# Gate columns of a hybrid layer computed in other places of the program: out of the first projection, into the joins and the last gated-delta steps

## The reference, cut to what matters

```python
h = rms_norm(x, norm_g[layer])
cols = split_columns(h @ w_in[layer])      # 'gate' is the first 1024 of 3448 columns
y_gdn = gdn_branch(cols, ...)              # gated delta rule, both directions
y_mla = mla_branch(cols, ...)
y_rwkv = rwkv7_branch(cols, ...)
mix = concatenate([y_gdn, y_mla, y_rwkv]) * silu(cols['gate'])
x = x + mix @ w_out[layer]
```

```python
u = u0_c - w_c @ s
o = qg_c @ s + p_c @ u
s = ge_c * s + kd_c.T @ u
```

## Time and profile before

| what | value |
|---|---|
| median of 3 runs | 4808.96 us (4803.95 to 4815.57) |
| the profiled execution, its own time | 4815.59 us |
| its span, first to last instruction | 4813.8 us |
| mean granted TensorE clock | 0.893 |
| TensorE (PE) busy | 4066.1 us, 84% |
| VectorE (DVE) busy | 2108.3 us, 44% |
| ScalarE (ACT) busy | 1239.2 us, 26% |
| GpSimd (POOL) busy | 275.6 us, 6% |

### The profile page before, as it was taken

The page is one execution under the profiler, slowest core; times in us unless marked ns, Lnnn a source line. Parts: engine busy times, 40 slices in busy tenths (PEclk is TensorE's granted clock), DMA queues, the critical chain, the costliest instruction groups (busy, mean ns, idle before and its releaser), DMA issues. The chain is left out here.

```text
span 4813.8 us, 51714 instructions
## 1 busy us (share of the span) xinstructions
PE 4066.1 (84%) x20488; PEld 2632.0 (55%) x20488; DVE 2108.3 (44%) x3647; ACT 1239.2 (26%) x2039; POOL 275.6 (6%) x236
## 2 busy tenths in 40 slices
PE   6847887898879694788789887849999999899999
PEld 4336634775664443663477565437777666344443
DVE  1266136554454127613665445325666667200001
ACT  2043134423332114313442434131111111210002
POOL 0011000000000001100000000001122111000000
PEclk9977698887999896779887898979999999999999
DMA  3220102112012212020301202231111110311120
GB/s 122 70 100 27 65 26 68 36 50 83 7 46 105 95 64 93 27 69 26 89 22 40 83 7 77 95 101 36 40 40 40 36 40 9 131 35 40 39 83 35
DMA packets 270405, 276.38 MB, mean 57 GB/s; under 512 B 11808, under 2 KB 241312, under 8 KB 270128
## 3 DMA queue, kind: packets, MB, share of 16 engines
q1 hardware_dynamic: 270192, 273.44, 17.2%
HBM read 199.54 MB, written 78.05 MB: 58 GB/s over the span
## 5 line engine op out<-in xcount | busy, mean ns | idle before, releaser
L3151 PE MATMUL ps<-hT,wr 128*128 128x512 f32 x768 | 333.2, 596 | 19.6 <-DMA wr<-in_w_in 19.6
L2940 DVE SCALAR_TENSOR_TENSOR cv<-glu,params,cv 128x1024 f32<-128x1024 f32 x240 | 338.5, 1410 | 6.1
L491 PE MATMUL ps<-hT,w_cols_g 128*128 128x512 f32 x576 | 261.9, 616 | 71.5 <-PEq L156 71.5
L3151 PEld LDWEIGHTS ps<-hT,wr 128*128 128x128 f32 x768 | 146.8, 191 | 205.3 <-issue 184.8
L491 PEld LDWEIGHTS ps<-hT,w_cols_g 128*128 128x128 f32 x576 | 113.7, 199 | 217.3 <-issue 217.3
L2337 PE MATMUL ps<-kT,qs 96*128 96x512 f32 x384 | 199.9, 650 | 34.2 <-DVE qs L2395 34.2
L2613 PE MATMUL ps<-w_out,mT 128*128 128x512 f32 x512 | 222.4, 593 | 0.0
L491 PE MATMUL ps<-hT,w_cols 128*128 128x512 f32 x448 | 196.1, 600 | 29.4 <-PEq L156 29.4
L2359 PEld LDWEIGHTS ps<-V,pT 128*128 128x128 f32 x1536 | 184.9, 192 | 56.5 <-issue 41.4
L3271 DVE TENSOR_TENSOR zs<-zs,ps 128x1024 f32<-128x1024 f32 x16 | 19.5, 1221 | 407.7 <-PE ps L3151 407.7
L2359 PE MATMUL ps<-V,pT 128*128 128x64 f32 x1536 | 183.5, 273 | 13.3 <-DVE om L2393 11.6
(11 more groups left out here) (478 smaller groups left out, 7452.9 us busy)
## 6 DMA issues: line engine op xcount, KB each, us to landing
fh<-hT_hbm SPq DMA_DIRECT2D x32, 512.0 KB, 4.5
x<-x_hbm SPq DMA_DIRECT2D x25, 512.0 KB, 6.9
w_cols_g<-in_w_in SPq DMA_DIRECT2D x24, 512.0 KB, 3.8
wr<-in_w_in SPq DMA_DIRECT2D x24, 512.0 KB, 3.8
hT_hbm<-hT SPq DMA_DIRECT2D x2, 4096.0 KB, 13.2
kb_raw_w<-kb_hbm SPq DMA_DIRECT2D x32, 256.0 KB, 3.2
hT<-hT_hbm SPq DMA_DIRECT2D x2, 4096.0 KB, 13.0
gate_in<-gate_hbm SPq DMA_DIRECT2D x8, 1024.0 KB, 8.4
```

What stands on the lines that cost most here:

```text
L491: m = pe.matmul(ps[:, 2 * (n % 3) + b, :], lhsT=wc[:, k, :], rhs=hT[:, k, P + b * 512:P + (b + 1) * 512], start=(k == 0), stop=(k == KD - 1))
L2940: vec.scalar_tensor_tensor(out=cv[:, h % 2, :], in0=src, scalar=w, in1=cv[:, h % 2, :], op0=ALU.mult, op1=ALU.add).then_inc(*VEC(f"tap{h}_ ...
L3151: q = pe.matmul(ps[:, two_banks(j) + b, :], lhsT=wr[:, j % NW, k, :], rhs=x_in[:, k, b * HALF:(b + 1) * HALF], start=(k == 0), stop=(k == ...
```

## The change

The gate product of 256 columns leaves `front`, with its weights' load, its copy and its store. The narrow product has two banks instead of one, and ScalarE computes the scales of group 1 before it copies narrow tiles 0 and 1. In `gdn_chunk` six fills instead of eight stand before each join, and the products of the other two stand one by one between the join's small products, one ahead of every three of those. The 256 gate columns are computed in steps 4 to 7, two tiles in each (`last_columns`, 8 products a tile), in four parts per step: four products ahead of `second_half`, four ahead of `to_state`, eight ahead of `out_of_chunk`. In steps 0 to 3 the turned keys are made after both `diff`, and VectorE makes kd of them after `across` instead of before it.

```diff
@@ front
                         scales(0)
+                        scales(1)
                         narrow(0)
                         narrow(1)
-                        scales(1)
                         scales(2)
@@ front, tensor
-                        narrow(0)
-                        narrow(1)
                         for t in range(NT):
+                            narrow(t)
                             if t + 2 < NT:
                                 turn(t + 2)
-                            gate(t)
-                            if t + 2 < NT:
-                                narrow(t + 2)
@@ TURNS
-                        TURNS += [f"gam{s + 1}", f"kt{s}", f"d{s + 4}_0", f"d{s + 4}_1", f"q{s}_0", f"q{s}_1", f"g{s + 4}_0", f"o{s}", f"g{s + 4}_1"]
+                        TURNS += [f"gam{s + 1}", f"d{s + 4}_0", f"d{s + 4}_1", f"kt{s}", f"q{s}_0", f"q{s}_1", f"g{s + 4}_0", f"o{s}", f"g{s + 4}_1"]
                     TURNS += ["pc1_0", "pc1_1", "of1_0", "of1_1"]
                     for s in range(4, NT):
-                        TURNS += ([f"gam{s + 1}"] if s < NT - 1 else []) + [f"kt{s}", f"q{s}_0", f"q{s}_1", f"o{s}"]
+                        TURNS += ([f"gam{s + 1}"] if s < NT - 1 else []) + [f"kt{s}", f"q{s}_0", f"q{s}_1", f"o{s}", f"f{s}"]
@@ new function, tensor
+                            def last_columns(s, part):
+                                b = claim(f"f{s}") if part == 0 else pair_of_banks(f"f{s}")
+                                n = 2 * NT + 2 * (s - 4) + part // 2
+                                if part == 0:
+                                    pe.wait_ge(*DMA.upto("fw", 3))
+                                if part % 2 == 0:
+                                    pe.wait_ge(*DMA.upto(f"fh{n % 2}", n // 2 + 1))
+                                for k in range(4 * (part % 2), 4 * (part % 2) + 4):
+                                    q = pe.matmul(ps[:, b + part // 2, 0:REST], lhsT=fh[:, n % 2, k, :], rhs=fw[:, k, 0:REST], start=(k == 0), stop=(k == KD - 1))
+                                if part % 2:
+                                    q.then_inc(*PE(f"fill{n}"))
@@ join, the same in its second half with NT * b + NT - 1
                                     for n in range(12):
+                                        if n % 3 == 0:
+                                            fill(NT * b + NT - 2, 4 * hf + n // 3, 4 * hf + n // 3 + 1)
                                         q = pe.matmul(ps[:, at, 32 * n:32 * n + 32], lhsT=AT5[:, 12 * hf + n, :], rhs=G[:, 0, :, 12 * hf + n], start=True,
@@ steps 0 to 3, tensor
                                 decays(s + 1)
-                                keys(s)
                                 diff(s + 4, 0)
                                 first_half(s)
                                 diff(s + 4, 1)
+                                keys(s)
                                 across(s)
@@ steps 4 to 7, tensor
                                 out_of_state(s)
+                                last_columns(s, 0)
                                 second_half(s)
                                 if s < NT - 1:
                                     values_in(s + 1)
+                                last_columns(s, 1)
                                 to_state(s)
+                                last_columns(s, 2)
+                                last_columns(s, 3)
                                 out_of_chunk(s)
@@ scalar: a copy of both tiles at once, after second_half and before out
+                            def last_columns(s):
+                                n = 2 * NT + 2 * (s - 4)
+                                act.wait_ge(*PE[f"fill{n + 1}"])
+                                for m in range(2):
+                                    act.wait_ge(*DMA.upto(f"fo{m}", n // 2))
+                                b = pair_of_banks(f"f{s}")
+                                act.copy(fo[:, :, 0:REST], ps[:, b:b + 2, 0:REST]).then_inc(*ACT(f"f{s}"))
@@ sync: the weights of the last columns are loaded behind the last fill, and their tiles two ahead
+                                    if n == NT * (c + 1) - 1:
+                                        fill_weights(c + 1)
+                                    fill_tile(n + 2)
```

More of the change, by code:

```diff
@@ L436, in _ @@
                         turned(1)
-                        for t in range(NT):
-                            if t + 2 < NT:
-                                normed(t + 2)
-                                turned(t + 2)
-                            gate(t)
+                        for t in range(2, NT):
+                            normed(t)
+                            turned(t)
                     @block.tensor
@@ L455, in narrow @@
                             pe.wait_ge(*VEC[f"h{t}_1"])
-                            if t:
-                                pe.wait_ge(*ACT[f"tm{t - 1}"])
+                            if t >= 2:
+                                pe.wait_ge(*ACT[f"tm{t - 2}"])
                             for k in range(KD):
-                                q = pe.matmul(ps[:, NARROW, 0:TM_W], lhsT=hT[:, k, (t + 1) * P:(t + 2) * P], rhs=wt[:, k, :], start=(k == 0), stop=(k == KD - 1))
+                                q = pe.matmul(ps[:, narrow_bank(t), 0:TM_W], lhsT=hT[:, k, (t + 1) * P:(t + 2) * P], rhs=wt[:, k, :], start=(k == 0), stop=(k == KD - 1))
                             q.then_inc(*PE(f"tm{t}"))
[L462 to L469, removed]
                         turn(0)
@@ L1546, in claim @@
                                     pe.wait_ge(*VEC["PT" + old[1:]])
+                                elif old is not None and old[0] == "f":
+                                    pe.wait_ge(*ACT[old])
                                 elif old is not None and old[0:2] == "kt":
@@ L1552, in claim, with fill @@
                                 return pair_of_banks(name)
[L1554 to L1563, removed]
-                                    q = pe.matmul(ps[:, WB + n % 2, 0:FILL], lhsT=fh[:, n % 2, k, :], rhs=fw[:, k, :], start=(k == 0), stop=(k == KD - 1))
-                                q.then_inc(*PE(f"fill{n}"))
+                            def fill(n, k0, k1):
+                                if k0 == 0:
+                                    pe.wait_ge(*DMA.upto("fw", n // NT + 1))
+                                    pe.wait_ge(*DMA.upto(f"fh{n % 2}", n // 2 + 1))
+                                    if n == NT:
+                                        pe.wait_ge(*ACT["w2_3"])
+                                        pe.wait_ge(*VEC["w2_3"])
+                                        pe.wait_ge(*VEC["S3"])
+                                    if n >= 2:
+                                        pe.wait_ge(*ACT[f"fill{n - 2}"])
+                                for k in range(k0, k1):
+                                    q = pe.matmul(ps[:, WB + n % 2, 0:FILL], lhsT=fh[:, n % 2, k, :], rhs=fw[:, k, :], start=(k == 0), stop=(k == KD - 1))
+                                if k1 == KD:
+                                    q.then_inc(*PE(f"fill{n}"))
@@ L1700, in join @@
                                     for n in range(12):
+                                        if n % 3 == 0:
+                                            fill(NT * b + NT - 1, 4 * hf + n // 3, 4 * hf + n // 3 + 1)
                                         q = pe.matmul(ps[:, at, 32 * n:32 * n + 32], lhsT=AT5[:, 12 * hf + n, :], rhs=RY[:, 0, :, 12 * hf + n], start=True,
@@ L1715, in _ @@
                             values_in(0)
-                            for n in range(NT):
-                                fill(n)
+                            for n in range(NT - 2):
+                                fill(n, 0, KD)
                             join(0)
@@ L1735, in _ @@
                                 pairs(s + 4, 1, 3)
-                            for n in range(NT, 2 * NT):
-                                fill(n)
+                            for n in range(NT, 2 * NT - 2):
+                                fill(n, 0, KD)
                             join(1)
```

51 lines of the change are left out of this document (28 added, 23 removed).

## The result

The changed kernel took 4814.73 us (median of 20 runs, 4803.49 to 4835.82); the kernel before, run beside it, 4801.73 (20 runs, 4768.22 to 4818.82). The ratio is 1.0031, with a 95% interval of 1.0015 to 1.0046: slower by 0.3%, where 4752 was forecast, 0.988 of before.

A forecast was written before the change was run, and what follows sets the result against it. Bounds taken: TensorE in `front` and joins, fills before joins, waits in steps 0 to 3, half clock in the last steps. Per layer -31.6 + 1.7 - 13.4 + 14.8 = -28.5, -57 in all: 4752 us, range 4715 to 4803.

The forecast's parts named there:

- Front: In `front`, the gate product's 28.3 us leave and a 3.5 us pause replaces one of 6.8: -31.6 us a layer.
- Starts of the joins: In `gdn_chunk`, six fills ahead instead of eight let the first join start 4.5 us earlier, the second 2.5.
- Joins: Length of each join in `gdn_chunk` with two fills moved in: 26 us, half clock for the first 10; bounds 23 and 42.
- the joins stay at half clock: Rival: joins take 42 us instead of 26, nothing gained behind; 75 us for four, 4827 us; chance 0.08, two joins only 0.12.
- Clock gained behind a join: Work right behind each join starts at full clock instead of half: 2.7 us gained, twice a layer.
- Steps 0 to 3: In `gdn_chunk`, later keys and kd shorten three steps by 4.0 us each and step 0 by 1.4: -13.4 us a layer.
- bring nothing: Rival on the turned keys in steps 0 to 3: same VectorE operations, kd only delays another copy; 4779 us, chance 0.08.
- Steps 4 to 7: In `gdn_chunk`, new gate products take 7.07 us a step, partly paid by a higher clock: +14.8 us a layer.

The follow-up runs named there:

- the lumps: The changed kernel with each join's two interleaved fills as four pieces of four products, one ahead of each quarter of the small products, pause kept: 4749.35 us, 0.9894 of before.
- kernel of keys, interleaving and repeated products: The kernel before, with keys later, two fills between each join's small products, and 17 and 16 extra overwritten fill products ahead of the joins: 4769.55 us, 0.9932.

## Why the prediction was wrong, step by step

**Front** was right: 33.2 us a layer for 31.6, with the one pause of 3.3 us where 3.5 was forecast.

**Starts of the joins** were right: -5.2 for -4.5 in the first, -2.6 for -2.5 in the second.

**Joins: this is the step that failed.** "I take 26, low for the first 10 us, nearer to the fills, since two fill instructions outweigh six small ones." They measured 41.1, low from first to last, in all four joins, near the upper bound of 42; the price at full clock was right as well (21 for 21.1). The level of the clock was wrong, not the cost at either level. The reasoning weighed the time that each kind takes. The row behind it, eight fills in a row that recovered the clock within a few us, is a row of *unbroken* fills, and by the lumps a piece of eight such instructions does recover it. A piece of two between pieces of six small ones does not, in sixteen repetitions. So of the two neighbouring rows the low one was the nearer, and the rival "the joins stay at half clock" should have had the larger chance. Its price was well put: 75 for four joins, and by the table's rows on the joins 34.8 a layer, 70 in all. Its time, 4827, is 12 above the measured 4815.

On pauses, these rows agree with the Trainium skill (TensorE: Matmul & The Clock Gate, "HAM oscillation — how this bites in real kernels"), which lets the clock fall back in a wait between bursts, so that each next burst starts low. What the prediction drew from the Trainium skill (TensorE: Matmul & The Clock Gate, "Why this matters for your kernels"), that sustained matmul work restores it, holds for the lumps. But that section asks only that TensorE be kept busy, and here 39.66 us of unbroken TensorE work stayed at 0.50; where the two differ, the measurement decides.

**Clock gained behind a join** was 0 for 2.7 twice, since it rested on the join; with the joins at full clock step 0 takes 19.2 instead of 22.4.

**Steps 0 to 3** were right: -12.8 for -13.4. The chain of nine operations is 9.3 us for 9.6, and steps 1 and 2 last 20.4 for 20.6. The keys alone gave the same in these steps, and with columns moved and fills ahead the kernels with old and new keys differ by 0.50% (0.9941 and 0.9891), 24 us for the 27 forecast. That they "bring nothing" is refuted.

**Steps 4 to 7** came out near the forecast (+11.9 and +14.7 for +14.8), but partly by luck. The base, 85.1 us, was one draw of the clock: the same 937 instructions took 64.4, 67.0, 75.7 and 85.2 us in other kernels. The prediction took 20.5 us of low clock in it as a property of the kernel that the new products would repair. On a base at or near full clock the new products add 31 to 34 us (98.5 against 67.0 and 64.4), about what `front` gives, and the kernel with columns moved and fills ahead (4747.59) is only 6 us from the one with the keys alone (4753.35), in one comparison. Moving them at the same clock is nearly neutral. What made steps 4 to 7 slow in the profile of before, and not with the keys alone, was not settled: the joins ahead of them are alike.

**The rest of the sum** fits what was measured once the joins are repaired: the kernels whose joins keep or regain the clock, all but one join of one of them, gave 0.9875, 0.9907 and 0.9894 of before, where 4752 is 0.988. With the last steps right partly by luck, this agreement is in part luck too.

## What to carry to other kernels

Do not spread dense matmul work between small products behind a pause: spread, it doubled the join's time, and in one piece the join took 24 us instead of 41. And ask first whether it has to move at all: left ahead of the pause, where it ran at full clock, it cost no more than in the lumps (255.5 us to step 4 against 255.9). Before an engine's work is reordered for overlap, look at which granted clock it will start, and whether what stands there has ever brought the clock back in the trace. And treat the length of a stretch whose mean clock lies between the two levels as one draw; read it in more than one trace before a term rests on it.

## What the runs showed of the hardware

- A mixture of six instructions of 32 columns and two of 384 keeps the clock at which it begins: 20.4 us at 2.4 GHz, 39.7 at 1.2, with the engine busy all the time in both. From the first small product on it did not change level in any of the 24 joins in the traces of the six kernels that had it, 15 at full clock and 9 at half.
- Eight fill instructions in a row, behind 9.32 us of pause, brought 2.4 GHz back, and so did the first lump in all twelve joins of the three kernels with lumps. Behind a pause of 2.95 us the clock fell within the join's first fill product (1.23 us, between 0.88 at full and 1.62 at half); behind pauses of 0.28 and 1.00 it stayed.
- The 96 small instructions alone take 19.0 us near half clock, with their weight loads busy 18.93 of it. At full clock, between lumps, they take about 11 (2.93 and 2.77 for 24 each).
- The untouched `rw_chunk`, with the same 1744 matmul instructions, takes different times in the two layers of one run (kernel of keys, interleaving and repeated products):

```profile
287.60:578.00 290.40, 203.71 (x1744) 177.15 (x1744) 151.35 (x336) 91.61 (x224) 31.18 (x42) 0.69 0.16 50
1809.70:2080.70 271.00, 183.68 (x1744) 159.10 (x1744) 151.28 (x336) 91.48 (x224) 31.27 (x42) 0.75 0.17 53
```

  VectorE and ScalarE are busy for the same time in both; TensorE and its clock differ. Why the clock differs was not settled. Such differences, of 10 to 20 us, are as large as what most edits here move.
